# Full-height score matmuls with copied heads, and a rearranged projection start in the second block's second layer

## Time and profile before

| | |
|---|---|
| median of three runs | 2213.84 us |
| the profiled execution, its own time | 2220.79 us |
| its span, first to last instruction | 2219.0 us |
| mean granted TensorE clock | 0.929 |
| TensorE busy | 1858.0 us (84%) |
| VectorE busy | 1351.6 us (61%) |
| ScalarE busy | 838.8 us (38%) |
| score loops | from 121.7 and 1014.2 us |
| Gated DeltaNet layer | from 1915 us to the end |

### The profile page before, as it was taken

The page is one execution under the profiler, slowest core; times in us unless marked ns, Lnnn a source line. Parts: engine busy times, 40 slices in busy tenths (PEclk is TensorE's granted clock), DMA queues, the critical chain, the costliest instruction groups (busy, mean ns, idle before and its releaser), DMA issues. The chain is left out here.

```text
span 2219.0 us, 22791 instructions
## 1 busy us (share of the span) xinstructions
PE 1858.0 (84%) x7428; PEld 1169.7 (53%) x7428; DVE 1351.6 (61%) x3102; ACT 838.8 (38%) x2309; POOL 674.8 (30%) x586
## 2 busy tenths in 40 slices
PE   7999887787887787799989788878778886899797
PEld 6967643343333222696764334333323265799796
DVE  6657857657657645665776756766755555384732
ACT  4341343343343433434134433434434355264231
POOL 4000354354444442400025534445444300000320
PEclk9969999999999999995999999899999997898998
DMA  6426899999999999542679999999999942352001
GB/s 236 136 79 265 327 421 421 421 421 421 421 422 421 421 422 380 210 140 77 257 295 421 421 421 421 421 421 421 421 421 421 418 143 85 116 180 96 1 1 48
DMA packets 107687, 660.92 MB, mean 298 GB/s; under 512 B 11953, under 2 KB 13361, under 8 KB 41649
## 3 DMA queue, kind: packets, MB, share of 16 engines
q0 software_dynamic: 73728, 536.90, 58.4%
q1 hardware_dynamic: 33840, 122.56, 15.6%
HBM read 658.37 MB, written 1.05 MB: 297 GB/s over the span
## 5 line engine op out<-in xcount | busy, mean ns | idle before, releaser
L621 PE MATMUL banks<-big 128*128 128x512 f32 x1680 | 810.5, 626 | 207.8 <-ACT big L834 207.4
L1166 DVE SCALAR_TENSOR_TENSOR big<-big 128x1024 bf16<-128x1024 f32 x420 | 509.2, 1224 | 402.4 <-DMA big<-in_experts,big 401.7
L910 POOL DMA_INDIRECT big<-in_experts,big x420 | 464.9, 1107 | 902.1 <-PE banks L621 545.5
L621 PEld LDWEIGHTS banks<-big 128*128 128x128 f32 x1680 | 315.1, 197 | 686.1 <-ACT big L834 367.1
L826 ACT ACTIVATE big<-big 128x1 f32<-128x1 f32 x512 | 101.9, 199 | 554.6 <-DVE big L1166 548.9
L834 ACT ACTIVATE big<-constants,big 128x128 f32<-128x128 f32 x512 | 205.6, 402 | 60.9 <-PE banks L621 14.0
L621 PE MATMUL banks<-expert_rows,big 128*128 128x512 f32 x368 | 175.1, 610 | 28.9 <-ACT big L834 28.9
L1166 DVE SCALAR_TENSOR_TENSOR big<-expert_rows,big 128x1024 bf16<-128x1024 f32 x92 | 112.0, 1225 | 79.7 <-DMA expert_rows<-in_experts,big 79.6
L830 ACT ACTIVATE big<-big 128x1 f32<-128x1 f32 x512 | 150.8, 294 | 17.6
L910 POOL DMA_INDIRECT expert_rows<-in_experts,big x92 | 111.3, 1210 | 126.7 <-PE banks L621 86.8
L1470 PE MATMUL banks<-x_parts,chunk_parts 128*128 128x256 f32 x1104 | 140.0, 290 | 4.8 <-DVE chunk_parts L1460 4.8
(11 more groups left out here) (361 smaller groups left out, 2184.2 us busy)
## 6 DMA issues: line engine op xcount, KB each, us to landing
big<-in_ada SPq DMA_DIRECT2D x48, 512.0 KB, 8.2
weight_ring<-in_w_in SPq DMA_DIRECT2D x40, 512.0 KB, 4.2
weight_ring<-in_gdn_in SPq DMA_DIRECT2D x32, 512.0 KB, 3.7
weight_ring<-in_wq SPq DMA_DIRECT2D x24, 512.0 KB, 7.8
weight_ring<-in_w_out SPq DMA_DIRECT2D x16, 640.0 KB, 4.2
weight_ring<-in_lru_in SPq DMA_DIRECT2D x16, 512.0 KB, 4.1
big<-in_experts,big POOLq DMA_INDIRECT x420, 20.8
expert_rows<-in_wq SPq DMA_DIRECT2D x8, 512.0 KB, 6.2
```

The source lines that it names most:

```text
L621: last = nc.tensor.matmul(sums_e[tt][:, c * 512:(c + 1) * 512], diag[:, v % NDIAG], rows_e[v % NBUF][:, D + c * 512:D + (c + 1) * 512], st ...
L910: nc.gpsimd.indirect_dma_start(rows_e[v % NBUF], None, d_e, bass.IndirectOffsetOnAxis(ap=expert[:, h, tt, a:a + 1], axis=0)).then_inc(arri ...
L1166: nc.vector.scalar_tensor_tensor(waste[:, v % 2], rows_e[v % NBUF][:, 0:D], 1.0, x_rows[:, tt], ALU.mult, ALU.mult, accum_out=dots[:, v:v ...
```

## The change

Scores: ScalarE copies each query tile once for each head, multiplied by a 0/1 column that keeps the rows of that head (`bd32`, `bd64`), into `alone` (the dead buffer `sq`) and `alone_m` (the dead memory tiles of `proj`). TensorE multiplies this copy with the whole key tile, 128 rows. VectorE raises `qk_ready` after every tile; ScalarE copies two heads between the roots and the SiLU, and the other heads at the top of units 1 to 6.

Gated DeltaNet: tiles 0 and 1 in plain f32 (`FIRST = 2`), the rate columns after tile 3, their exponentials and sigmoid on ScalarE before tile 8's evacuation, squares in pairs, and the sums of a pair (8 records) after tiles 13, 15, ... 27.

```diff
@@ TensorE, first block
-                pe.wait_ge(s("qk_ready"), 1)
+                pe.wait_ge(s("qk_ready"), 4)
...
+                    if 2 <= u < 4:
+                        pe.wait_ge(s("qk_ready"), 2 * u + 2)
...
-                            rows = slice(DH * h, DH * (h + 1))
-                            last = nc.tensor.matmul(out[:, j * T:(j + 1) * T], qk[rows, j, qt * P:(qt + 1) * P], qk[rows, 2 + j],
+                            pe.wait_ge(s("alone_ready"), 2 * h + j + 1)
+                            last = nc.tensor.matmul(out[:, j * T:(j + 1) * T], alone[:, 2 * h + j, qt * P:(qt + 1) * P], qk[:, 2 + j],
...
-                            last = nc.tensor.matmul(out[:, j * T:(j + 1) * T], qk[rows, 4 + h // 2, j * P:(j + 1) * P],
-                                                    qk[rows, 6 + h // 2], start=True, stop=True)
+                            pe.wait_ge(s("alone_ready"), 2 * HEADS + h + 1)
+                            last = nc.tensor.matmul(out[:, j * T:(j + 1) * T], alone_m[:, h, j * P:(j + 1) * P],
+                                                    qk[:, 6 + h // 2], start=True, stop=True)
@@ ScalarE, first block
+                def alone_keep(h):
+                    if h < HEADS:
+                        for j in range(2):
+                            nc.scalar.activation(alone[:, 2 * h + j], qk[:, j], ACT.Copy, scale=bd32[:, h:h + 1]).then_inc(s("alone_ready"), 1)
+                    else:
+                        act.wait_ge(s("qk_ready"), KD)
+                        nc.scalar.activation(alone_m[:, h - HEADS], qk[:, 4 + (h - HEADS) // 2], ACT.Copy,
+                                             scale=bd64[:, h % 2:h % 2 + 1]).then_inc(s("alone_ready"), 1)
+                act.wait_ge(s("qk_ready"), 2)
+                for h in range(2):
+                    alone_keep(h)
...
                 for u in range(12):
+                    if 1 <= u < 7:
+                        alone_keep(u + 1)
@@ gdn_layer, TensorE (rates() and pair_sums(p) hold the old loops)
             for n in range(NQ):
...
+                if n < FIRST:
+                    wt = tile_of(n)
+                    for k in range(KD):
+                        pe.wait_ge(s("xn_ready"), k + 1)
+                        last = nc.tensor.matmul(ps[n % 4][:, 0:T], wt[:, k], xn[:, k], start=(k == 0), stop=(k == KD - 1))
+                    last.then_inc(s("used"), 1)
...
+                if n == RATES_AT:
+                    rates()
+                if n == SUMS_AT:
+                    pe.wait_ge(s("ab_kept"), 1)
+                if n >= SUMS_AT and (n - SUMS_AT) % 2 == 0 and (n - SUMS_AT) // 2 < LH:
+                    last = pair_sums((n - SUMS_AT) // 2)
@@ gdn_layer, ScalarE
+                if n == RATES_AT + 5:
+                    act.wait_ge(s("sp_in"), 1)
+                    nc.scalar.activation(w4[0], w4[0], ACT.Exp).then_inc(s("sp_exp"), 1)
+                    nc.scalar.activation(small[:, 248:256], par[:, Q_ALOG:Q_ALOG + LH], ACT.Exp).then_inc(s("alog_exp"), 1)
+                    act.wait_ge(s("ab_kept"), 1)
+                    nc.scalar.activation(beta, bb, ACT.Sigmoid).then_inc(s("beta_ready"), 1)
...
+                    if 0 < done <= 2 * LH:
+                        act.wait_ge(s("silu"), done)
+                        nc.scalar.activation(sq[:, done - 2:done], qkv[:, done - 2:done], ACT.Square).then_inc(s("sq_qk"), 1)
                     done += 2
-                    if done == 2 * LH:
-                        act.wait_ge(s("silu"), 2 * LH)
-                        nc.scalar.activation(sq, qkv[:, 0:2 * LH], ACT.Square).then_inc(s("sq_qk"), 1)
@@ gdn_layer, VectorE (n == RATES_AT + 3 holds the old reading of the rates)
+            for n in range(FIRST, NQ):
+                chunk_low(nc, dve, s, split, ring, n, FIRST)
+                if n == RATES_AT + 3:
+                    dve.wait_ge(s("ab_done"), 1)
```

More of the change, by code:

```diff
@@ L299, in first_block @@
     cat_sq = proj[:, 0:KMIX]
+    alone, alone_m = sq, proj[:, N_MQ:N_MQ + HEADS]
     def part_low_wait(engine, j):
@@ L494, in _ @@
                             h = u - 8
-                            rows = slice(MH * (h % 2), MH * (h % 2 + 1))
-                            last = nc.tensor.matmul(out[:, j * T:(j + 1) * T], qk[rows, 4 + h // 2, j * P:(j + 1) * P],
-                                                    qk[rows, 6 + h // 2], start=True, stop=True)
+                            pe.wait_ge(s("alone_ready"), 2 * HEADS + h + 1)
+                            last = nc.tensor.matmul(out[:, j * T:(j + 1) * T], alone_m[:, h, j * P:(j + 1) * P],
+                                                    qk[:, 6 + h // 2], start=True, stop=True)
                     last.then_inc(s("scores_ready"), 1)
@@ L1011, in _ @@
                     gain = par[:, C_QG + i // 2:C_QG + i // 2 + 1]
-                    last = nc.vector.scalar_tensor_tensor(qk[:, i], src, gain, nc_ps[4 + i // 2][:, (i % 2) * T:(i % 2 + 1) * T],
-                                                          ALU.mult, ALU.mult)
-                last.then_inc(s("qk_ready"), 1)
+                    nc.vector.scalar_tensor_tensor(qk[:, i], src, gain, nc_ps[4 + i // 2][:, (i % 2) * T:(i % 2 + 1) * T],
+                                                          ALU.mult, ALU.mult).then_inc(s("qk_ready"), 1)
                 dve.wait_ge(s("lam_exp"), 1)
@@ L1567, in gdn_layer @@
     NG = NPAIR // GRP
+    RATES_AT, SUMS_AT = 3, 13
+    FIRST = 2
     def grp(v, q):
@@ L1576, in _ @@
             for n in range(N_END):
-                if n >= R2:
-                    sy.wait_ge(s("lo_done" if n - R2 < NQ else "used"), n - R2 + 1)
+                if FIRST <= n - R2 < NQ:
+                    sy.wait_ge(s("lo_done"), n - R2 - FIRST + 1)
+                elif n >= R2:
+                    sy.wait_ge(s("used"), n - R2 + 1)
                 src = d_in[n] if n < NQ else d_out[n - NQ]
@@ L1599, in _, with rates, pair_sums @@
             norm_pe(nc, pe, s, ps[4][:, 0:T], sq, ones)
[L1600 to L1606, removed]
+            def rates():
+                pe.wait_ge(s("xn_ready"), KD)
+                pe.wait_ge(s("ab_loaded"), 16)
+                for tt in range(NT):
+                    for k in range(KD):
+                        last = nc.tensor.matmul(ps[5][:, 16 * tt:16 * (tt + 1)], xn[:, k, tt * P:(tt + 1) * P], wab[:, k],
+                                                start=(k == 0), stop=(k == KD - 1))
+                last.then_inc(s("ab_done"), 1)
+            def pair_sums(p):
+                pe.wait_ge(s("sq_qk"), p + 1)
+                for tt in range(NT):
+                    for i in (2 * p, 2 * p + 1):
+                        last = nc.tensor.matmul(ps[5][:, 32 + 16 * tt + i:33 + 16 * tt + i], sq[:, i, tt * P:(tt + 1) * P], ones[:, 0:1],
+                                                start=True, stop=True)
+                return last
             for n in range(NQ):
@@ L1609, in _ @@
                     pe.wait_ge(s("kept"), n - 3)
-                chunk_product(nc, pe, s, ps[n % 4][:, 0:T], split, xr, n).then_inc(s("used"), 1)
+                if n < FIRST:
+                    wt = tile_of(n)
+                    for k in range(KD):
+                        pe.wait_ge(s("xn_ready"), k + 1)
+                        last = nc.tensor.matmul(ps[n % 4][:, 0:T], wt[:, k], xn[:, k], start=(k == 0), stop=(k == KD - 1))
+                    last.then_inc(s("used"), 1)
+                else:
+                    chunk_product(nc, pe, s, ps[n % 4][:, 0:T], split, xr, n, FIRST).then_inc(s("used"), 1)
+                if n == RATES_AT:
[4 more added lines that the diff above has]
+                    last = pair_sums((n - SUMS_AT) // 2)
+                    if (n - SUMS_AT) // 2 == LH - 1:
+                        last.then_inc(s("sum_qk"), 1)
                 if n == 3 * LH + 4:
@@ L1616, in _ @@
                     last.then_inc(s("gc_done"), 1)
[L1618 to L1623, removed]
             pe.wait_ge(s("gc_kept"), 1)
@@ L1761, in _ @@
             modulate_act(nc, act, s, xn, cd)
[L1762 to L1769, removed]
+            for n in range(FIRST, FIRST + SPLITS):
+                chunk_high(nc, act, s, split, ring, n, FIRST)
             act.wait_ge(s("pads"), 1)
@@ L1779, in _ @@
                     nc.scalar.activation(zs[:, n - 3 * LH], ps[n % 4][:, 0:T], ACT.Silu).then_inc(s("kept"), 1)
-                if n + SPLITS < NQ:
-                    chunk_high(nc, act, s, split, ring, n + SPLITS)
+                if FIRST + SPLITS <= n + SPLITS < NQ:
+                    chunk_high(nc, act, s, split, ring, n + SPLITS, FIRST)
                 if n >= 6 and n % 2 == 1 and done < 3 * LH:
@@ L1866, in _ @@
             x_parts(nc, dve, s, xr, xn)
[L1868 to L1878, removed]
+            for n in range(FIRST, NQ):
+                chunk_low(nc, dve, s, split, ring, n, FIRST)
+                if n == RATES_AT + 3:
+                    dve.wait_ge(s("ab_done"), 1)
```

(6 more changed lines are left out.)

## The result

The changed kernel takes 2187.77 us, the median of four runs (2186.35 to 2188.23), against 2215.78 us for the kernel before in four runs on the same chip. The ratio is 0.9872, its 95% interval 0.9858 to 0.9886: 28.0 us are gone, and the prediction of 2190.5 us (2181 to 2205) holds. The profiled execution took 2187.52 us.

What follows compares the result with a forecast made beforehand. No engine bounds the whole; TensorE at its low clock bounds the score loops, on one serial chain. 12.6 + 10.7 = 23.3 us off 2220.79 gives 2197.5 for the profiled execution, 2190.5 for the median, range 2181 to 2205.

Steps and rivals of the forecast that it cites:

- The clock: Score loops: full rows keep TensorE's clock up, its unit falling from 3.05 to 1.6 to 1.8 us.
- The size of the loop: Score loops: 6.3 us gained a layer, 12.6 us for both, with steps of at most 1.92 us.
- the dip: Score loop behind unit 3: TensorE idles 3 us, the clock may fall; 1.7 us lost, ends 0 and 3.
- The first maximum's loss: Score loop: four copies ahead of SiLU move the first maximum from 125.30 to about 126.9, 1.6 us lost.
- start: Last layer's projection: tile 2 follows the norm's first matmul sooner, 17.65 instead of 25.98 us; 7.7 us gained.
- rates: Projection: rate matmuls come back after tile 3, 3.5 us at the upper clock, perhaps lowering it; 4.5 us lost.
- ScalarE's stall: Projection: exponentials and sigmoid before tile 8's evacuation need table loads; 1.3 us lost, ends 0 and 3.8.
- sums: Projection: 64 records between tiles 13 and 27, where TensorE bounds, cost 7.2 us without holding the clock down.
- behind tile 31: Projection's end: VectorE's next step comes 4.4 instead of 15.9 us later; 11.5 us gained.
- tile 27: Projection: TensorE's wait for VectorE falls from 4.58 to about 1.7 us; 4.5 us gained, ends 0 and 6.3.
- Rival B: Loops and projection: no clock falls, no ScalarE stall, tile 27's wait gone; 2180 us, 13%.
- Rival C: Projection: sums between tiles pull the clock down for product tiles from 13 on; slower, 2234 us, 5%.

Runs made afterwards that it cites:

- experiments 2 and 3: Changed kernel with only the score matmuls narrowed to 32 or 64 rows: all heads 0.9964 of the kernel before, memory heads alone 0.9913, differential heads alone 0.9906.
- after_again: The changed kernel itself, measured again on one chip beside the version with two ScalarE moves: 2187.88 us, 0.9877 of the kernel before.
- experiment 5: Changed kernel with the eight pairs of sums back behind tile 31 in one loop, squares still in pairs: 0.9905 of the kernel before.
- diff_strip: Changed kernel with the eight differential units on 32 rows again, the four memory units on full rows: 0.9906 of the kernel before.

## Why the prediction was right

- **The clock** was the step on which the sum rested, and it held: full rows bring it to 1.00, and narrow ones alone take it away (experiments 2 and 3). The clock was 0.50 at 4.00 of 4.00 us busy with narrow rows and 1.00 at 3.01 busy with full ones. The Trainium skill ("TensorE: Matmul & The Clock Gate", Part 1) lets the clock follow how busy the PE has been. For this loop the measurement decides against that, at least for busy time as the profile counts it, with modelled ends. At equal clock a narrow unit loses 0.43 to 0.48 us. The Trainium skill ("TensorEngine Tiling (Array Packing)", Key Properties) says that changing the tiling mode drains TensorE. The loss fits that, but no run here tells a drain from another cost of narrow tiles.
- **The size of the loop** was too small: 6.3 us a layer forecast, 10.3 and 11.1 measured. From first to last maximum I had 18.7 and 1.7 for the dip, 20.4; it was 18.1. The step is 1.78, not 1.92 us, because VectorE's instructions start some 0.1 us before the modelled end of the one ahead, which adding durations misses (six steps, 0.8 us); the last step is 1.48 (0.4); the dip cost 3.0 - 1.9 = 1.1 us (0.6); the first combination came 0.3 earlier. And the part behind the last maximum gained 3.4, not 1.7: from the last maximum to the conv product 5.2 became 4.35 us, from there to the second L406 15.1 became 12.6. I had priced the conv product alone (1.97 us after, as foreseen), and not what stands behind it. The first maximum's loss of 1.6 us came as forecast.
- **The projection** came to 10.5 us, forecast 10.7, with these terms against the forecast: start 7.4 (7.7); rates -5.1 (-4.5), 3.5 for themselves and 1.6 because the clock dips behind them (the next seven tiles take 21.89 us, while three later ones take 8.7, or 2.9 each); ScalarE's stall 1.16 (1.3), at tile 11, through the parts as described; sums -6.9 (-7.2); behind tile 31, 11.2 (11.5); tile 27 about 3.2 (4.5), since it still ran partly at the low clock, 4.24 us for 24 records. These make 8.6, and the norm-to-L1943 distance shows 8.0. The remaining 2.5 us lie behind L1943, where the prediction had nothing, so that the total is met is in part luck. They have no fixed place: in the profile of `after_again` the distance to the matmul ahead of L1943 was 125.2 instead of 126.9 us and the rest 167.8 instead of 165.9, with the sum again 293.0, and tile 27 ran at the upper clock (3.11 us for its 24 records instead of 4.24). Where the clock falls in these stretches shifts between executions.
- **The total.** 23.3 us forecast, 28.0 measured by medians, 31.9 by stages. The missing size is the loops', 8.8 us by the stages. That the median came within 3 us of 2190.5 is partly luck: the sum gives 2197.5 for the profiled execution, and the one after took 2187.52, 10 us less, but the profiled execution of before lay 7 us above the median of 2213.84 and the one after at its median, and that makes up for 7 of the 10. Rival B's time (2180) was passed only by removing the loops' dips with ScalarE's order. Rival C needed the clock to fall over product tiles from 13 on: the six pairs of tiles from 14 to 25 take 5.99 us each, at the upper clock throughout, and the one dip comes behind tile 27's wait. In one piece the same sums do lower it (experiment 5).

Open is what about a narrow matmul counts. Experiments 2 and 3 change the number of rows and the tiling mode together, and none had narrow rows without a change of mode. That the full-height one-column sums lower the clock as well shows only that a change of mode isn't needed for it. The rows that the change adds hold zeros, so rows without useful numbers count as well; other fillings weren't tried. Open is also what sets the time until the clock is back: behind the first loop of the kernel before, TensorE had full rows from 151.83 us on, with pauses of 0.47 and 0.77 us, and stayed at 0.50 until 162, while in `diff_strip` the third unit with full rows had it back.

## What to carry to other kernels

Where TensorE is 100% busy at a granted clock of 0.50, look at the shape of its matmuls before anything else: a copy with zeros on an idle engine, which fills all rows, cost here some 0.45 us a piece on ScalarE, and the rows it fills saved 19 us in two stages. Break up long runs of narrow work (one or sixteen columns) between wide tiles, and don't put them behind a wait. When a bound is removed, follow the next one by start times of successive instructions, and look at which engine's order makes the new pause: two moves on ScalarE gave another 12 us.

## What the runs showed of the hardware

- 32- and 64-row f32 matmuls between full-height transposes brought the clock from 1.00 to 0.50 with TensorE 3.46 to 4.00 of 4.00 us busy; in `diff_strip` it came back in the third unit with full rows. I had expected the rows to matter, but not that the fall follows within two units of 64 rows.
- Thirty-two matmuls of 16 columns at the full clock lower it behind them: 3.64 us for themselves, and 1.6 us more in the wide tiles that follow. With the rates elsewhere these tiles show no dip.
- One-column sums take 0.81 us for 8 records in pieces and 11.74 us for 64 in one run: the pieces cost 6.9 us together, 4.8 less than that run and 2.5 less than the 9.37 of the kernel before.
